# Digit codes for the one-hots, first picks among the last dense tiles, other shares of weighing, six dot products handed over

## The chip, the cores and the metric

The kernel runs on one core of a Trainium2 chip. The time is device microseconds of one execution, and the metric is the median over runs. Engine names are those of the profile: PE is TensorE (PEld its weight loads), DVE is VectorE, ACT is ScalarE, POOL is GpSimd, and SP is SyncE, which here only issues DMAs.

## What is computed

One layer on 256 tokens of width 2048: a modulated norm, an input projection, an RWKV-7 group beside a short convolution, an output projection, and then the PEER feed-forward, a mixture of 16,384 tiny experts. Only the last is touched:

```python
v1, i1 = lax.top_k(s1, PEER_TOPK)                # 16 of 128 first keys, per token and head
v2, i2 = lax.top_k(s2, PEER_TOPK)                # 16 of 128 second keys
cidx = i1[..., :, None] * N_KEYS + i2[..., None, :]
top, pos = lax.top_k(cand, PEER_TOPK)            # 16 experts of 8 heads: 128 per token
gate = jax.nn.softmax(top, axis=-1)
u = jnp.take(expert_u, idx, axis=0)
act = jax.nn.gelu(jnp.einsum('td,tkd->tk', h_t, u), approximate=False)
vv = jnp.take(expert_v, idx, axis=0)
return jnp.einsum('tk,tkd->td', g * act, vv)
```

## The kernel before

All work is written out by hand, engine by engine, with semaphores; each engine runs its own list in order. The feed-forward goes through four stages.

**Dense u stage.** Each expert row u has 2048 columns. The first 896 are multiplied densely for all experts: 128 tiles (`u_dense`, 448 KB each), tile j holding the experts whose second key is j, seven matmuls per tile (L1330); ACT copies each result to `dense` (L842). SP loads the tiles (`product_tile`, L450): ten of them (`KEPT`) early into spare memory, the others into four slots, each load waiting for the product that frees its slot. The other 1152 columns are fetched by gather: POOL issues one indirect DMA for each of 256 rows n = (block of 128 tokens, k) (L599) into a ring of six slots, and gather n waits until `u_dot` says that dot n-6 is done. DVE routes (`route`) and makes the dots (`dots`, L1794), 198 of them (`LATE`) before it turns to the next stage.

**Pick stage.** 64 iterations q of four tokens. PE spreads the four tokens' first keys over the partitions (`spread_keys`, L1344, four bf16 matmuls), ACT makes of them a one-hot with two operations (`one_hot`: Abs L857, Relu L859), PE multiplies the one-hot with `dense` (`key_rows`, L1356) and transposes it (`turn_one_hot`, L1363), ACT keeps the transposed one (L868), and DVE picks the products from PSUM (`pick`, L1802, four). In 58 of the iterations DVE also makes one of the remaining dots. Once block 0 is picked (q = 32), gelu and gate give its weights. From q = 36 on DVE, and in parallel POOL, write weighted one-hots for group q-36 (`weigh`, L1847 and L615, two tokens of four each; in block 1, POOL one of four), PE multiplies them in iteration q = group + 37 (`token_weights`, L1385), and ACT stores the result (L873). PE's order in an iteration is `spread_keys(q+1)`, `key_rows(q)`, `turn_one_hot(q)`, `token_weights(q-37)`. POOL's part of group j stands behind gather 232+j (`WEIGH_AT`), so it is issued after dot 226+j.

**Drain.** After the 64 iterations: groups 27 to 63 of the weighing, without picks.

**Dense v stage.** 128 tiles of `v_dense` (1104 columns) are multiplied on PE (L1413) while DVE sums 256 gathered rows of the other 944 columns (L1863).

## Time and profile before

| | |
|---|---|
| median of 3 runs | 1931.37 us (1931.03 to 1933.72) |
| the profiled execution's own time | 1930.16 us |
| its span, first to last instruction | 1928.4 us |
| busy: PE, DVE, ACT, POOL | 1833.6, 1317.2, 389.7, 750.5 us |
| mean granted clock of PE | 0.985 |
| HBM | 315 GB/s over the span |

The profile gives, per group of instructions, busy time, mean duration, and the idle time before them with what ended it; a chain that ended last; timelines; and busy time by windows. A busy share is a mean over stages, so the stages are read one by one.

### The profile page before, as it was taken

The numbers are of one execution on the slowest core, as the hardware profiler recorded it, in microseconds if no ns is written. First come the engines' busy times: TensorE is split into PE (matmuls) and PEld (weight loads), VectorE is DVE, ScalarE is ACT, GpSimd is POOL, SyncE is SP. The second block draws the span as 40 slices with busy tenths as digits, with TensorE's granted clock in tenths as the row PEclk, the third lists the DMA queues.
The fourth block names the chain that finished last, engine by engine and source line by source line (L and its number), as shares of the span: only waits on it lengthen the run. The fifth ranks groups of instructions, "written<-read, shape, count | busy, mean of one in ns | idle before, by whom it ended". The sixth has DMA issues, their size and how long they took to land.

```text
span 1928.4 us, 28418 instructions
## 1 busy us (share of the span) xinstructions
PE 1833.6 (95%) x10929; PEld 1415.7 (73%) x10929; DVE 1317.2 (68%) x2611; ACT 389.7 (20%) x842; POOL 750.5 (39%) x789
## 2 busy tenths in 40 slices
PE   3899999999999999999999999888989999999997
PEld 3787787777875458888888888778876666656664
DVE  5855666666662333598999975799986666666666
ACT  3022222222222020011111111588740000000001
POOL 2002212222111000365444443338895786744552
PEclk8789999999999999999999999999999999999999
DMA  9956656765581954989999999876449999999997
GB/s 396 420 200 263 228 197 248 292 249 210 213 345 54 402 204 157 370 323 410 405 407 402 402 410 409 327 230 205 144 154 408 409 409 408 409 408 409 409 406 284
DMA packets 124382, 609.09 MB, mean 316 GB/s; under 512 B 15584, under 2 KB 15712, under 8 KB 101216
## 3 DMA queue, kind: packets, MB, share of 16 engines
q1 hardware_dynamic: 66496, 330.33, 44.0%
q0 software_dynamic: 57344, 274.76, 37.3%
q8 instruction: 87, 1.43, 0.3%
q10 hardware_dynamic: 416, 2.25, 0.3%
q14 instruction: 39, 0.32, 0.0%
HBM read 603.09 MB, written 4.19 MB: 315 GB/s over the span
## 4 chain that ended last, share of the span: by engine, by line
PE 81%; DVE 8%; DMA 7%; issue 2%; POOL 2%; ACT 1%; DVEq 0%; SPq 0%; ACTq 0%
PE ps L1413 22%; PE ps L1330 20%; PE ps L996 14%; PE ps L1045 6%; PE ps L1235 6%; DMA arena<-in_v_dense 3%; PE ps L1084 3%; DVE arena L1474 2%; DVE ps L1802 2%; PE ps L1385 2%; DVE arena L1794 2%; DMA arena<-in_ada 2%; POOL arena L615 2%; DMA arena<-in_w_in 1%; PE ps L1356 1%
## 5 line engine op out<-in xcount | busy, mean ns | idle before, releaser
L1413 PE MATMUL ps<-arena 128*128 128x368 f32 x1536 | 477.4, 473 | 7.7 <-DMA arena<-in_v_dense 7.0
L1413 PEld LDWEIGHTS ps<-arena 128*128 128x128 f32 x1536 | 300.9, 196 | 182.8 <-DMA arena<-in_v_dense 10.9
L1863 DVE SCALAR_TENSOR_TENSOR arena<-arena 128x944 f32<-128x944 f32 x254 | 305.2, 1201 | 173.7 <-DMA arena<-in_v_rows,arena 172.3
L599 POOL DMA_INDIRECT arena<-in_u_rows,arena x256 | 257.6, 1006 | 346.6 <-DVE arena L1794 287.2
L1330 PE MATMUL ps<-arena 128*128 128x256 f32 x1792 | 386.9, 379 | 0.0
L1330 PEld LDWEIGHTS ps<-arena 128*128 128x128 f32 x1792 | 340.5, 190 | 46.1
L599 POOL DMA_INDIRECT arena<-in_v_rows,arena x256 | 295.7, 1155 | 182.3 <-DVE arena L1863 149.4
L996 PE MATMUL ps<-arena 128*128 128x256 f32 x1440 | 349.4, 386 | 2.6 <-DMA arena<-in_w_in 2.6
L1794 DVE SCALAR_TENSOR_TENSOR arena<-arena,ps 128x1152 f32<-128x1152 f32 x208 | 277.8, 1349 | 52.8 <-DMA arena<-in_u_rows,arena 52.2
L996 PEld LDWEIGHTS ps<-arena 128*128 128x128 f32 x1440 | 261.8, 190 | 40.6 <-DMA arena<-in_w_in 4.2
L1453 DVE SCALAR_TENSOR_TENSOR arena<-arena 128x2048 f32<-128x2048 f32 x60 | 143.5, 2392 | 24.8 <-DMA arena<-in_ada 24.7
L842 ACT ACTIVATE arena<-ps 128x256 f32<-128x256 f32 x128 | 52.0, 406 | 336.6 <-PE ps L1330 336.6
L1045 PE MATMUL ps<-arena 128*128 128x512 f32 x256 | 115.4, 598 | 0.0
L1235 PE MATMUL ps<-arena 128*128 128x256 f32 x512 | 111.4, 379 | 0.0
L1235 PEld LDWEIGHTS ps<-arena 128*128 128x128 f32 x512 | 96.9, 190 | 13.0
L725 ACT ACTIVATE arena<-ps 128x256 f32<-128x256 f32 x152 | 55.7, 383 | 200.9 <-PE ps L1084 139.0
L572 POOL TENSOR_TENSOR arena<-arena 128x256 f32<-128x256 f32 x40 | 39.1, 978 | 130.7 <-PE ps L1084 95.0
L1356 PE MATMUL ps<-arena 128*128 128x128 f32 x512 | 72.2, 281 | 12.7 <-DVE ps L1802 9.9
L1045 PEld LDWEIGHTS ps<-arena 128*128 128x128 f32 x256 | 47.0, 190 | 50.5 <-issue 49.4
L1474 DVE SCALAR_TENSOR_TENSOR arena<-arena 128x512 f32<-128x512 f32 x112 | 75.0, 745 | 10.6 <-DMA arena<-in_ada 10.4
L615 POOL TENSOR_SCALAR arena<-arena 128x128 f32<-128x128 f32 x96 | 78.1, 822 | 8.4 <-PE ps L1385 6.6
L1084 PEld LDWEIGHTS ps<-arena 64*64 64x64 f32 x2112 | 50.4, 133 | 39.6 <-issue 35.0
(251 smaller groups left out, 1746.0 us busy)
## 6 DMA issues: line engine op xcount, KB each, us to landing
arena<-in_ada SPq DMA_DIRECT2D x96, 1024.0 KB, 7.4
arena<-in_v_dense SPq DMA_DIRECT2D x128, 552.0 KB, 8.7
arena<-in_u_dense SPq DMA_DIRECT2D x128, 448.0 KB, 7.1
arena<-in_w_in SPq DMA_DIRECT2D x45, 1024.0 KB, 7.3
arena<-in_w_tail SPq DMA_DIRECT2D x32, 1024.0 KB, 9.1
arena<-in_w_in SPq DMA_DIRECT2D x12, 512.0 KB, 16.6
arena<-in_u_rows,arena POOLq DMA_INDIRECT x256, 10.1
arena<-in_v_rows,arena POOLq DMA_INDIRECT x256, 11.7
```

Source lines behind the costliest of these rows:

```text
L599: nc.gpsimd.indirect_dma_start(out=row, out_offset=None, in_=table[:, :], in_offset=bass.IndirectOffsetOnAxis(ap=i32(idx[:, b, k:k + 1]), ...
L615: last = nc.gpsimd.tensor_scalar(pick_w[q % len(pick_w)][i], iota, idx2T[:, t:t + 1], wT[:, t:t + 1], ALU.is_equal, ALU.mult)
L996: last = mm(bank(b, 0, T), w[:, k, :], hT[:, k, :], start=(k == 0), stop=(k == KC - 1))
L1045: return mm(bank(OUT_BANKS[g][b]), yT[:, OUT_K[n], b * P:(b + 1) * P], w, start=(n == 0), stop=(n == KC - 1))
L1084: last = mm(out(w, a, q), l(HALVES[w], a, q), r(HALVES[w], a, q), start=True, stop=True)
L1235: last = mm(bank(b0 + s // 2, (s % 2) * T, (s % 2) * T + T), w[:, kk, s * P:(s + 1) * P], h2T[:, k, :], start=(k == 0 and s % 2 == 0), sto ...
L1330: last = mm(bank(5 + j % 2, 0, T), w[:, k, :], h2T[:, k, :], start=(k == 0), stop=(k == KU - 1))
L1413: last = mm(sums(b)[:, g, :], dense[:, b, j // 2, :, j % 2], w[:, g * VG:(g + 1) * VG], start=(j == 0), stop=(j == NKEYS - 1))
L1453: ins = stt(dst, ring[:, slot, :], silu_c[:, k:k + 1], dst, ALU.mult, ALU.add)
L1474: v0.done(stt(a, row, silu_c[:, k:k + 1], a, ALU.mult, ALU.add), name)
L1794: stt(row, row, 1.0, h, ALU.mult, ALU.mult, accum_out=actv[:, b, k:k + 1]).then_inc(u_dot, 1)
L1863: stt(total[b], row, w, total[b], ALU.mult, ALU.add).then_inc(v_sum, 1)
```

## The change

In words, part by part:

- **Codes.** The first key is written as two digits (hi = key/16, lo = key mod 16) and their squares, in bf16: `make_digits` on DVE (eight small operations per block), saved to a DRAM tensor `first_key_codes` by two ACT DMAs before tile 112's copy. `code_tile(q)` on SP loads them back, 4 partitions x 4 x 256 bytes, one DMA per iteration, 64 in all, into two code tiles of eight used rows. One matmul with constant weights (`code_w`, made on POOL; bias by `make_bias` on DVE) and one Relu now give the one-hot. SP's list has the code tiles behind the last u tile and ahead of the first v tile; the v tiles also wait for `handed_sum`.
- **First picks.** PE transposes the second keys and does `spread_keys(0)` ahead of u tile 125, ACT copies them and makes one-hot 0 before the copy of tile 126, and the eight Exp of the gates stand before the copy of tile 112.
- **Kept tiles.** 14 instead of 10; six of these are loaded among the output projection's tiles.
- **Dots.** `LATE` is 202 instead of 198, and the pick stage holds 48 dots instead of 58: none in q = 0, 1, 5, 8, ..., 29, 31, 40, 47, 54, 61.
- **Handed dots.** The last six rows (k = 122 to 127 of block 1) are gathered by POOL into two other buffers, multiplied there with a copy of h (`h_copy`, ACT, in q = 1), and summed by ACT (q = 12, 17, ..., 37).
- **Weighing.** POOL's parts of groups 0 to 31 stand behind gathers 232 to 249, five for every four gathers; in block 1, POOL has one token in two groups of three and none in the third, where DVE does all four. The transpose of block 0's weights moves from q = 34 to 35.

PE at the end of the u tiles, before (L1330 tile products, L1335 second keys, L1344 spread, L1356 key rows, L1363 transposes):

```order
L1330 MATMUL ps<-arena 128x256 [waits u_tile_evacuated,u_tile_landed3]
L1330 MATMUL ps<-arena 128x256 x6
L1330 MATMUL ps<-arena 128x256 [waits u_tile_evacuated,u_tile_landed0]
L1330 MATMUL ps<-arena 128x256 x6
L1330 MATMUL ps<-arena 128x256 [waits u_tile_evacuated,u_tile_landed1]
L1330 MATMUL ps<-arena 128x256 x6
L1335 MATMUL ps<-arena 128x128 [waits experts_picked]
L1335 MATMUL ps<-arena 128x128
L1344 MATMUL ps<-arena 128x128 [waits u_row_multiplied]
L1344 MATMUL ps<-arena 128x128 x3
L1344 MATMUL ps<-arena 128x128 [waits one_hot_ready]
L1356 MATMUL ps<-arena 128x128 [waits one_hot_ready,u_tile_evacuated]
```

And the same place now (L1434 tile products, L1424 second keys, L1418 spread, L1446 key rows):

```order
L1424 MATMUL ps<-arena 128x128 [waits experts_picked]
L1424 MATMUL ps<-arena 128x128
L1418 MATMUL ps<-arena 128x512 [waits first_key_code_landed0,first_key_code_landed1,numbers_made,u_row_multiplied]
L1434 MATMUL ps<-arena 128x256 [waits u_tile_evacuated,u_tile_landed3]
L1434 MATMUL ps<-arena 128x256 x6
L1434 MATMUL ps<-arena 128x256 [waits u_tile_evacuated,u_tile_landed0]
L1434 MATMUL ps<-arena 128x256 x6
L1434 MATMUL ps<-arena 128x256 [waits u_tile_evacuated,u_tile_landed1]
L1434 MATMUL ps<-arena 128x256 x6
L1418 MATMUL ps<-arena 128x512 [waits one_hot_ready]
L1446 MATMUL ps<-arena 128x128 [waits one_hot_ready,u_tile_evacuated]
```

Three tile products now stand behind a matmul that waits for two code tiles to land. SP's list there, now (before, the v tiles followed the u tiles at once):

```order
L452 DMA arena<-in_u_dense 128x896 [waits u_tile_product] x110
L508 DMA arena<-first_key_codes 4x4x128 [waits first_key_digits_saved,code_tile_zeroed]
L508 DMA arena<-first_key_codes 4x4x128 x3
L508 DMA arena<-first_key_codes 4x4x128 [waits first_keys_spread]
L508 DMA arena<-first_key_codes 4x4x128
...
L517 DMA arena<-in_v_dense 128x1104 [waits u_tile_product,handed_row_summed]
```

The code tiles are issued behind every u tile. POOL from gather 227 on, now (L631 gathers, L673 weighing, two tokens a group):

```order
L682 TENSOR_TENSOR arena<-arena 128x1152 [waits handed_row_landed1]
L631 DMA arena<-in_u_rows,arena 128x1152 [waits u_row_multiplied] x6
L673 TENSOR_SCALAR arena<-arena 128x128 [waits turned_weights_evacuated]
L673 TENSOR_SCALAR arena<-arena 128x128
L631 DMA arena<-in_u_rows,arena 128x1152 [waits u_row_multiplied]
L673 TENSOR_SCALAR arena<-arena 128x128 x2
```

Group j's weighing on POOL still starts behind gather 232, as before; but the dot that gather 232 waits for has moved. DVE's list around its first weighing (group 0, q = 36), before:

```order
L1794 SCALAR_TENSOR_TENSOR arena<-arena,ps 128x1152 [waits u_row_landed5]
L1802 SCALAR_TENSOR_TENSOR ps,arena<-arena,ps 128x128 [waits key_rows_ready]
L1802 SCALAR_TENSOR_TENSOR ps,arena<-arena,ps 128x128 x3
L1794 SCALAR_TENSOR_TENSOR arena<-arena,ps 128x1152 [waits u_row_landed0]
L1847 TENSOR_SCALAR arena<-arena 128x128 [waits turned_weights_evacuated]
L1847 TENSOR_SCALAR arena<-arena 128x128
```

and now:

```order
L1914 SCALAR_TENSOR_TENSOR arena<-arena,ps 128x1152 [waits u_row_landed3]
L1922 SCALAR_TENSOR_TENSOR ps,arena<-arena,ps 128x128 [waits key_rows_ready]
L1922 SCALAR_TENSOR_TENSOR ps,arena<-arena,ps 128x128 x3
L1914 SCALAR_TENSOR_TENSOR arena<-arena,ps 128x1152 [waits u_row_landed4]
L1974 TENSOR_SCALAR arena<-arena 128x128 [waits turned_weights_evacuated]
L1974 TENSOR_SCALAR arena<-arena 128x128
```

Row n lies in slot n mod 6: the dot ahead of weighing 0 was number 228 (slot 0) and is now number 226 (slot 4). The core of the diff:

```diff
@@ SP
+                if n in EARLY_KEPT:
+                    keep_tile(EARLY_KEPT[n])
...
+            def code_tile(q):
+                b, t = divmod(4 * q, P)
+                if q == 0:
+                    sp.wait_ge(code_zero, 2)
+                    sp.wait_ge(digits_saved, 16 * TB)
+                if q >= 4 and q % 2 == 0:
+                    sp.wait_ge(spread, q - 2)
+                rows = code[q // 2 % 2][4 * (q % 2):4 * (q % 2) + 4, :]
+                sp.dma_start(rows.rearrange("r (t k) -> r t k", t=4), codes[b, t:t + 4].rearrange("t r k -> r t k")).then_inc(code_land[q % 4], 16)
+            for q in range(T // 4):
+                code_tile(q)
+            sp.wait_ge(handed_sum, HANDED)
@@ POOL
+            def hand(i):
+                if i:
+                    pool.wait_ge(handed_land[(i - 1) % 2], 16 * ((i - 1) // 2 + 1))
+                    row = handed_row[(i - 1) % 2]
+                    nc.gpsimd.tensor_tensor(row, row, h_copy, ALU.mult).then_inc(handed_mul, 1)
+                else:
+                    pool.wait_ge(tile_ps, NKEYS)
+                    pool.wait_ge(h_kept, 1)
+                if i < HANDED:
+                    if i >= 2:
+                        pool.wait_ge(handed_sum, i - 1)
+                    gather(handed_row[i % 2], u_rows, 1, KTOP - HANDED + i, handed_land[i % 2])
...
-                if n >= WEIGH_AT:
-                    weigh(n - WEIGH_AT)
+                if n in HAND_AT:
+                    hand(HAND_AT.index(n))
+                while n >= WEIGH_AT and weighed < min(5 * (n - WEIGH_AT + 1) // 4, P // 4):
+                    weigh(weighed)
+                    weighed += 1
@@ ACT
-                h = hot[q % 2].rearrange("p a b -> p (a b)")
-                nc.scalar.activation(h, bank(0), ACT.Abs, bias=minus_p).then_inc(hot_out, 1)
-                act.wait_ge(hot_out, 2 * q + 1)
-                nc.scalar.activation(h, h, ACT.Relu, bias=ones[:, 0:1], scale=-1.0).then_inc(hot_out, 1)
+                nc.scalar.activation(hot[q % 2].rearrange("p a b -> p (a b)"), bank(0), ACT.Relu, bias=one_minus).then_inc(hot_out, 1)
...
+                if q == 1:
+                    act.wait_ge(tile_ps, NKEYS)
+                    act.wait_ge(u_dot, LATE)
+                    nc.scalar.activation(h_copy, ps[:, GU:2 * GU], ACT.Copy).then_inc(h_kept, 1)
@@ PE
+            def spread_keys(q):
+                if q % 2 == 0:
+                    for n in range(2):
+                        pe.wait_ge(code_land[(q + n) % 4], 16 * (q // 4 + 1))
+                if q:
+                    pe.wait_ge(hot_out, q)
+                mm(bank(0), code_w[q % 2], code[q // 2 % 2], start=True, stop=True).then_inc(spread, 1)
@@ tables
-LATE = TB * KTOP - 58
-KEPT = tuple(24 + 6 * n for n in range(10))
+HANDED = 6
+NROWS = TB * KTOP - HANDED
+LATE = 202
+NO_DOT = (0, 1) + tuple(range(5, 32, 3)) + (31,) + (40, 47, 54, 61)
+HAND_AT = tuple(LATE + UROWS + 3 * i for i in range(HANDED + 1))
+SUM_AT = tuple(12 + 5 * i for i in range(HANDED))
+KEPT = tuple(18 + 6 * n for n in range(14))
+EARLY_KEPT = {8: 2, 10: 3, 12: 4, 14: 5, 16: 12, 18: 13}
...
-WEIGH_AT = TB * KTOP - 24
-POOL_TOKENS = ((2, 3), (3,))
+WEIGH_AT = 232
...
+def pool_tokens(q):
+    return (2, 3) if q < P // 4 else (3,) if q % 3 else ()
```

## Rows read from the trace of the kernel before

**Rows 1.** Busy time by windows: stretch, length, PE, PEld, DVE, ACT, POOL, clock, DMA, GB/s.

```profile
1100.00:1200.00 100.00, 100.00 (x465) 88.06 (x464) 68.98 (x125) 13.34 (x33) 40.28 (x43) 1.00 1.03 409
...
1260.00:1280.00 20.00, 16.77 (x154) 15.29 (x151) 20.00 (x91) 17.66 (x30) 7.36 (x8) 1.00 0.74 221
...
1340.00:1360.00 20.00, 19.11 (x170) 17.55 (x169) 20.00 (x85) 16.61 (x29) 18.55 (x22) 1.00 0.69 207
...
1500.00:1600.00 100.00, 100.00 (x385) 63.69 (x384) 65.05 (x55) 1.09 (x2) 82.37 (x55) 1.00 1.02 408
```

**Rows 2.** The chain that ended last, two pieces: start us, us, what.

```profile
840.96 386.79 PE ps L1330 x1792
...
1433.65 59.63 PE ps L1413 x192
```

**Rows 3.** Timeline, last dot ahead and first pick: start, us, engine, line, [idle before].

```profile
1224.97 1.35 DVE L1794 SCALAR_TENSOR_TENSOR arena<-arena,ps 128x1152 f32<-128x1152 f32 x1
...
1227.77 0.40 ACT L842 ACTIVATE arena<-ps 128x256 f32<-128x256 f32 x1 [2.62 <-PE ps L1330]
...
1230.84 1.13 PE L1356 MATMUL ps<-arena 128*128 128x128 f32 x8 [0.44 <-ACT arena L859]
...
1232.09 0.35 DVE L1802 SCALAR_TENSOR_TENSOR ps<-arena,ps 128x128 f32<-128x128 f32 x1 [5.76 <-PE ps L1356]
```

**Rows 4.** Timeline of SP's queue, the last six u tile loads.

```profile
1200.57 15.44 SPq L450 DMA_DIRECT2D arena<-in_u_dense  x6
```

**Rows 5.** DMA view, 1222 to 1223 us, SP's queue q1: packets, MB, share.

```profile
q1 hardware_dynamic: 2, 0.00, 1.0%
```

**Rows 6.** DMA view, 710 to 845 us: SP's store of x, KB, us to landing.

```profile
out<-arena SPq DMA_DIRECT2D x1, 2048.0 KB, 16.9
```

**Rows 7.** Timeline of DVE in an early iteration: first pick, dot, next pick.

```profile
1272.34 0.35 DVE L1802 SCALAR_TENSOR_TENSOR ps<-arena,ps 128x128 f32<-128x128 f32 x1
...
1273.42 1.35 DVE L1794 SCALAR_TENSOR_TENSOR arena<-arena,ps 128x1152 f32<-128x1152 f32 x1
...
1274.69 0.35 DVE L1802 SCALAR_TENSOR_TENSOR ps<-arena,ps 128x128 f32<-128x128 f32 x1
```

**Rows 8.** Timeline of one iteration with weighing, all engines.

```profile
1321.18 1.02 POOL L599 DMA_INDIRECT arena<-in_u_rows,arena  x1 [0.17 <-issue]
...
1321.49 1.35 DVE L1794 SCALAR_TENSOR_TENSOR arena<-arena,ps 128x1152 f32<-128x1152 f32 x1
...
1322.24 1.64 POOL L615 TENSOR_SCALAR arena<-arena 128x128 f32<-128x128 f32 x2
...
1322.77 0.59 DVE L1847 TENSOR_SCALAR arena<-arena 128x128 f32<-128x128 f32 x2
...
1323.29 0.34 DVE L1802 SCALAR_TENSOR_TENSOR ps<-arena,ps 128x128 f32<-128x128 f32 x1
...
1323.47 1.13 PE L1385 MATMUL ps<-arena 128*128 128x128 f32 x8
...
1324.66 1.11 PE L1356 MATMUL ps<-arena 128*128 128x128 f32 x8
```

**Rows 9.** Timeline, a dot and the gather that waited for it.

```profile
1305.04 1.35 DVE L1794 SCALAR_TENSOR_TENSOR arena<-arena,ps 128x1152 f32<-128x1152 f32 x1
...
1306.67 0.94 POOL L599 DMA_INDIRECT arena<-in_u_rows,arena  x1 [1.41 <-DVE arena L1794]
```

**Rows 10.** Timeline, multiplications of 256 columns on POOL, and DVE beside one.

```profile
417.09 2.34 DVE L1453 SCALAR_TENSOR_TENSOR arena<-arena 128x2048 f32<-128x2048 f32 x1
...
417.25 2.77 POOL L579 TENSOR_TENSOR arena<-arena 128x256 f32<-128x256 f32 x1 [0.36 <-DVE arena L1606]
...
420.09 0.61 POOL L581 TENSOR_TENSOR arena<-arena 128x256 f32<-128x256 f32 x1
```

**Rows 11.** Timeline, one-column matmuls of PE.

```profile
710.02 3.85 PE L929 MATMUL ps<-arena 128*128 128x1 f32 x32
```

**Rows 12.** Windows as in Rows 1: granted clock just behind.

```profile
713.00:717.00 4.00, 4.00 (x23) 4.00 (x23) 3.13 (x8) 2.55 (x9) 0.00 (x0) 0.57 0.99 371
```

More of the change, by code:

```diff
@@ L242, in build_layer @@
         idx2T = new(T)
-        ident_h = new(P // 2).bitcast(BF16)
-        idx1_h = [new(KTOP // 2).bitcast(BF16) for _ in range(TB)]
         actv, wv = new(TB, KTOP), new(TB, KTOP)
+        digit_at = [take(0) - TB * KTOP, take(2 * KTOP)]
+        digits = [view(a, 2 * KTOP).bitcast(BF16).rearrange("p (t k) -> p t k", t=4) for a in digit_at]
+        code_w = [ones[:, n * KTOP // 2:(n + 1) * KTOP // 2].bitcast(BF16) for n in range(2)]
         assert take(0) <= ring_at + 3 * SL
@@ L630, in _ @@
                 if n == 0:
-                    for q in range(TB * KTOP - WEIGH_AT, P // 4):
+                    for q in range(weighed, P // 4):
                         weigh(q)
@@ L1894, in _ @@
                     keep_weights(0)
[L1895 removed]
+                if q not in NO_DOT:
                     dots(ndot[0], ndot[0] + 1)
```

214 lines of the change are left out of this document (148 added, 66 removed).

## The prediction

> **What bounds the kernel now.** I read the chain that ended last first, then busy time by windows, then the timelines at the joints. The chain is PE's nearly everywhere: the u tiles are one unbroken piece of 386.79 us, 3.022 us a tile, from 840.96 to 1227.75, and the v tiles start at 1433.65 [rows 2]. The reader should see in the windows which stage leaves which engine room [rows 1]. In the u stage PE and the DMA engines are both full (409 GB/s) and DVE is idle for 31 of 100 us. In the early iterations of the pick stage DVE is full, at 20.00 of 20, and PE, ACT and POOL are not. In the iterations with weighing DVE is full, PE has 0.9 us left of 20 and POOL 1.5. In the v stage PE and DMA are full and the change touches nothing. So only the 205.9 us between the last u tile and the first v tile can move, and whatever delays a u tile is paid in full; the v stage follows with its 487 us unchanged, since its bytes, slots and order are the same.
>
> **Where the picks begin.** Between the last u tile and the first pick lie 4.3 us, in which DVE sits idle for 5.76 us and PE and ACT work on one-hot 0 [rows 3]. With one-hot 0 ready, what is left is ACT's last copy (0.40), the signal to PE (0.15) and the key rows (1.25 from start to pick): 1.8 us, a gain of 2.5. The first two iterations then have no dot, which takes 2 x 1.27 us from DVE [rows 7], but it can't use this: one-hot 2 stands on ACT behind the new copy of h, 1152 columns from PSUM, and pick 2 comes about 6.2 us after the last u tile against 9.1 now. Both together: **-2.9 us**.
>
> **Codes.** PE now waits ahead of tile 125 for code tiles 0 and 1. PE is there at 840.96 + 125 x 3.022 = 1218.7. SP issues them behind the last u tile, so not before 1216.0 [rows 4], and the last u tile's bytes leave SP's queue only at about 1222, after which it is empty [rows 5]. That a small transfer doesn't pass what stands ahead of it in SP's queue is seen earlier: the 2 MB store needs 16.9 us to land [rows 6], although 2 MB alone are 5 us at 409 GB/s, because four query tiles of 1 MB each stand ahead. So the codes land between 1222.1 and 1224; I take 1223.2, near the queue's end since they are small. With signal and spread (0.4 us) tile 125 starts at 1223.6 instead of 1218.7: **+4.9 us**, bounds 3.9 and 6.0 if the queue holds. PE is then idle for 4.5 us. Behind the nearest stretch of this kind, 3.85 us of one-column matmuls [rows 11], the granted clock fell to its lower level (1.2 GHz) and was 0.57 on average over the next 4 us [rows 12], that is some 3.4 us at half rate: **+1.7 us**, bounds 0 and 1.7; I take the upper end because the idle stretch is longer than that one.
>
> By the Trainium skill (DMA: Bandwidth & Descriptors, "Anatomy of one DMA") a transfer costs about 2.0 us plus its bytes, and by that alone the codes would land at about 1218.2 and PE would wait for nothing. The same page ("Queues, rings and completion order") says that each DMA engine takes the descriptors of a ring in order; by that rule, the trace agrees with its 16.9 us.
>
> **Dots.** An iteration with a dot takes DVE 1.08 us of picks and 1.27 of dot [rows 7]; with weighing, dot and two tokens take 1.80 [rows 8], in all 2.87. In iterations 2 to 31 there were 24 dots and are 20, and DVE is the full engine: 4 x 1.27 = **-5.1 us**. In block 1 four more iterations lose their dot, but there PE is full for 19.11 of 20 us, 2.74 of 2.87 [rows 1], and DVE must wait for its key rows: 0.13 each by the windows, at most about 0.3 by PE's gaps, **-1.0 us** with bounds -0.5 and -1.3. The four dots moved ahead of the picks bring 4 x 0.59 MB into the u stage and the four more kept tiles take 4 x 0.46 MB out of its DMA-bound part: 0.5 MB, 1.3 us at 409 GB/s. The last dot ahead of the picks ended at 1226.3 [rows 3] and ends near 1227.6, while PE's first picks aren't ready before 1234. Nothing, unless PE doesn't wait. The bias, digits and clearing on DVE (some 30 small operations, 6 us) lie in its idle 31 per cent. The six early kept tiles (6.6 us of DMA) load among the output projection's tiles, where PE has six slots ahead. The Relu that replaces two operations, and the one spread matmul for four, free ACT and PE, which aren't full in the early iterations: nothing.
>
> **Weighing on POOL.** This is the largest term. POOL's part of group j stands behind gather 232+j (five groups for four gathers), and gather n waits for dot n-6. Before, dot 226 was made in iteration 34 and group 0 was needed by PE in iteration 37. Now `LATE` is 4 higher, but 12 of the first 32 iterations have no dot instead of 6: dots 202 to 221 fill iterations 2 to 30, dot 222 falls on 32, and dot 226 on 36. So POOL can start on group 0 only behind the dot of iteration 36, and PE wants it in iteration 37, ahead of the key rows of iteration 38, for which DVE waits. The loop of two iterations is: gather starts 0.28 after the dot ends [rows 9], gather 1.02, two tokens 1.64, signal about 0.14 (an estimate, half of the 0.28), PE's weighing and spread 1.19 (1323.47 to 1324.66), key rows to pick 1.25, picks 1.08, dot 1.35 [rows 3, 7, 8], in all 7.95 us, against 2 x 2.87 = 5.74 us now. That is 2.2 us for every pair of groups whose POOL part has only one iteration's lead. Counted through the order, with five groups for four gathers and no dot at 40, 47, 54 and 61, those groups are 0, 1, 2, 3, 5, 6, 7, 8, 12 and 13; the others have two iterations and are on time. Five pairs: **+11.0 us**, bounds 8 (if some of the wait fits PE's gaps) and 13.
>
> **Handed dots.** Six multiplications of 1152 columns on POOL: 4.5 x 0.61 = 2.75 us each by the row without interference [rows 10], while POOL is busy for 7.4 of 20 us [rows 1]. Three rows take DVE 3 x 2.35 and one and a half iterations without a dot 1.6, 8.7 us, and POOL's work for them is 3 x 1.2 + 2.75 = 6.4. Hidden; uncovered from 5 us a multiplication. ACT's copies and sums (seven of about 1.2 us) lie in what the dropped Abs frees.
>
> **Drain.** POOL's share of block 1 falls to two thirds and DVE's rises by 11 tokens of 0.26 us; PE needs 0.90 us a group either way. I take -0.4, bounds 0 and -1.
>
> **Sum.** -2.9 + 4.9 + 1.7 - 5.1 - 1.0 + 11.0 - 0.4 = +8.2 us. The profiled execution, 1930.16 us, becomes 1938.4; the median lies 1.2 us above that execution, so the forecast is 1931.37 + 8.2 = **1939.6 us**. With all lower or all upper bounds at once: 1933 to 1944.
>
> **The rivals.** *The codes land in time*, because small descriptors get through between those of the u tile. For it: code tiles are 16 KB. Against it: [rows 6]. Then the 4.9 and 1.7 us go: 1933.0. *POOL is early enough*, because its lead is longer than I count. For it: POOL has slack in the early iterations. Against it: gather 232 can't be issued before its dot whatever POOL's slack. Then 1928.6. *Both*, which is the case on the other side: it decides at the point where the two delays together are below the 9.4 us that the picks gain, and with neither the time is 1939.6 - 17.6 = 1922.0, faster. *POOL's multiplications are held up by DVE*: one of 256 columns took 2.77 us instead of 0.61 while DVE worked on two operands in SBUF [rows 10]. Against it: the dots take one operand from PSUM, and POOL's weighing beside them kept its 0.82 us a token [rows 8]. At 8 us each, 6 x (3.6 + 8 - 8.7) = 17 us more: 1957. The Trainium skill (SBUF — State Buffer, "SBUF: two separate sides") says that a DVE operation with two SBUF inputs and a GpSimd operation exclude each other for their whole length; by that rule, the trace agrees with the 2.77 us, and the dots wouldn't hold POOL up.
>
> **How the numbers follow.** Forecast 0.50, codes in time 0.11, POOL early 0.16, both 0.15, multiplications held up 0.06, and 0.02 for the rest. The range takes in the forecast with its bounds and the second and third case, and leaves out most of the last two: 1925 to 1945. A measurement of this kernel tells about 0.2% (3.9 us) from no change. The cases at 1933.0 and 1928.6 lie within it, the latter not far from its edge: faster 0.18, same 0.25, slower 0.57.
>
> **What would show it.** A wait of 4 to 6 us of PE ahead of tile 125, ended by a DMA of the codes, and the granted clock behind it. First pick 1.8 us after the last u tile. Early iterations at 2.35 us with a dot and 1.08 without. Ten iterations from q = 36 to 49 in pairs of 7.9 us, with PE's weighing waiting for POOL (L673). The forecast is wrong if the u tiles end before 1229, or if PE never waits more than a few us in all for POOL's weighing.

## The result, and the profile after

The changed kernel takes 1946.92 us (median; 1945.24 to 1948.72) and the kernel before 1931.3 us beside it: the medians lie 15.6 us apart. The ratio is 1.0074 with a 95% interval of 1.0061 to 1.0087, which is 14.3 us. The forecast was 1939.6 us with a range of 1925 to 1945. The direction was right, the forecast change of 8.2 us was about half of what came, and the time lies 1.9 us above the range.

The profiled execution of the changed kernel has a span of 1945.9 us against 1928.4, 17.5 us more. The chain that ended last has again one piece per stage, but there is now a transfer in it (start us, length us, what; L1434 are the u tiles' products, L1476 the token weights, L1502 the v tiles):

```profile
839.46 374.70 PE ps L1434 x1736
1214.98 7.56 DMA arena<-first_key_codes
1223.27 11.51 PE ps L1434 x42
...
1449.79 59.63 PE ps L1502 x192
```

The u tiles, one piece of 386.79 us in [rows 2], are broken by a code tile of 4 KB that lands 7.56 us after it was issued (at 1222.54), and the three tiles behind it take 11.51 us, where three tiles before took 9.07. The v tiles start at 1449.79 instead of 1433.65. PE's timeline (start us, us, [idle before and what ended it]) and then the windows (columns as in [rows 1]; the eighth number is the granted clock) show both:

```profile
1217.01 0.38 PE L1424 MATMUL ps<-arena 128*128 128x128 f32 x2
1222.68 0.59 PE L1418 MATMUL ps<-arena 128*128 128x512 bf16 x1 [5.29 <-DMA arena<-first_key_codes]
1223.06 11.70 PE L1434 MATMUL ps<-arena 128*128 128x256 f32 x42
```

```profile
1220.00:1223.00 3.00, 0.32 (x1) 0.33 (x2) 2.05 (x5) 0.00 (x0) 1.20 (x2) 0.70 1.04 410
1223.00:1226.00 3.00, 3.00 (x8) 2.40 (x8) 2.87 (x5) 0.00 (x0) 2.01 (x3) 0.50 1.02 407
```

PE stood idle for 5.29 us; then it is busy for 3.00 of 3.00 us with 8 matmuls, at the lower level of its clock (0.50), where a window of the same length at 1.00 holds 15.

The first picks answer to [rows 3]. The last u tile ends at 1234.78 (1223.27 + 11.51); the picks of iterations 0, 1 and 2 (picks 0, 1 and 2 from here on) start 1.7, 3.2 and 5.7 us later, against 4.3, 6.7 and 9.1 before. On DVE's timeline:

```profile
1236.52 0.35 DVE L1922 SCALAR_TENSOR_TENSOR ps<-arena,ps 128x128 f32<-128x128 f32 x1 [9.78 <-PE ps L1446]
...
1237.99 0.36 DVE L1922 SCALAR_TENSOR_TENSOR ps<-arena,ps 128x128 f32<-128x128 f32 x1 [0.24 <-PE ps L1446]
...
1240.45 0.36 DVE L1922 SCALAR_TENSOR_TENSOR ps<-arena,ps 128x128 f32<-128x128 f32 x1 [1.24 <-PE ps L1446]
```

The handed multiplications, which [rows 10] could only scale to 2.75 us, are one group of the view by lines for 1240 to 1320 us (count, busy us, mean ns):

```profile
L682 POOL TENSOR_TENSOR arena<-arena 128x1152 f32<-128x1152 f32 x6 | 15.9, 2658 | 0.9 <-DMA arena<-in_u_rows,arena 0.8
```

Where weighing begins, the timeline reads quite unlike [rows 8]. L1914 is DVE's dot, L631 the gather, L673 POOL's weighing, L1476 PE's use of it, L1446 the key rows that DVE's next pick (L1922) needs:

```profile
1316.01 1.60 POOL L673 TENSOR_SCALAR arena<-arena 128x128 f32<-128x128 f32 x2
...
1317.66 2.07 PE L1476 MATMUL ps<-arena 128*128 128x128 f32 x8 [5.02 <-POOL arena L673]
...
1319.96 1.91 PE L1446 MATMUL ps<-arena 128*128 128x128 f32 x8
...
1321.91 0.36 DVE L1922 SCALAR_TENSOR_TENSOR ps<-arena,ps 128x128 f32<-128x128 f32 x1 [3.75 <-PE ps L1446]
...
1322.99 1.35 DVE L1914 SCALAR_TENSOR_TENSOR arena<-arena,ps 128x1152 f32<-128x1152 f32 x1
...
1324.62 0.99 POOL L631 DMA_INDIRECT arena<-in_u_rows,arena  x1 [4.08 <-DVE arena L1914]
...
1325.66 1.57 POOL L673 TENSOR_SCALAR arena<-arena 128x128 f32<-128x128 f32 x2
...
1327.28 0.97 PEld L1476 LDWEIGHTS ps<-arena 128*128 128x128 f32 x8 [1.87 <-POOL arena L673]
1327.28 1.16 PE L1476 MATMUL ps<-arena 128*128 128x128 f32 x8 [1.63 <-POOL arena L673]
...
1328.49 1.05 PE L1446 MATMUL ps<-arena 128*128 128x128 f32 x8
...
1329.59 0.35 DVE L1922 SCALAR_TENSOR_TENSOR ps<-arena,ps 128x128 f32<-128x128 f32 x1 [1.37 <-PE ps L1446]
```

Read from 1322.99 down, this is the loop that the prediction named: dot, gather (which had waited 4.08 us for it), two tokens on POOL, PE's weighing, the key rows, the next pick. Above it is the same loop with PE at half clock: its weighing takes 2.07 us instead of 1.16 and the key rows 1.91 instead of 1.05. The granted clock of that stretch, and PE's waits for POOL from 1300 to 1410 us (total us, times, longest):

```profile
1317.60:1321.90 4.30, 4.24 (x19) 4.08 (x20) 0.56 (x4) 1.18 (x2) 2.61 (x4) 0.50 0.72 242
```

```profile
PE ps L1476 <- POOL arena L673: 17.5, 11, 5.0
```

The starts of the first picks of all iterations, taken from DVE's timeline, give the whole pick stage. Iterations 37 and 38 take 10.04 us together, 39 and 40 take 7.70, 42 and 43 take 7.71, 44 and 45 take 8.88, 49 and 50 take 8.89, against 5.74 before: 14.5 us more in ten iterations. The others with weighing take 2.9 with a dot and 2.5 without, but for 57 to 60 with 3.0 to 3.2. The two pairs of 7.7 us have the clock at 1.00 throughout, although PE waits 2.55 us for POOL in one of them (first window below). In the pair of iterations 44 and 45 it falls 1.5 us after PE has resumed its work at 1346.05, behind a wait of 2.09 us (second window):

```profile
1338.40:1342.00 3.60, 3.40 (x27) 3.13 (x28) 1.75 (x11) 1.77 (x3) 2.61 (x3) 1.00 0.71 239
1347.60:1350.90 3.30, 3.30 (x18) 3.30 (x17) 1.94 (x9) 1.41 (x3) 2.86 (x4) 0.50 0.60 179
```

From the profiled execution of before to that of after, in us:

| stretch | before | after | change | forecast |
|---|---|---|---|---|
| start of the u tiles | 840.96 | 839.46 | -1.5 | 0 |
| u tiles, with the wait for the codes | 386.79 | 395.3 | +8.5 | +6.6 |
| last u tile to pick 2 | 9.05 | 5.67 | -3.4 | -2.9 |
| pick 2 to pick 36 | 75.03 | 71.88 | -3.1 | -5.1 |
| pick 36 to pick 63 | 78.06 | 91.77 | +13.7 | +10.0 |
| pick 63 to the first v tile | 43.76 | 45.69 | +1.9 | -0.4 |
| v tiles to the end | 494.75 | 496.1 | +1.4 | 0 |
| sum | | | +17.5 | +8.2 |

### The profile page after: what moved, and what is told of

Same layout as the page of the kernel before. It is cut to its first block, busy times and chain, and to the rows that moved or that the text cites. A ratio compares the mean times of both kernels' runs of the same rounds, so it can differ in the third digit from the quotient of the medians.

```text
span 1945.9 us, 28104 instructions
## 1 busy us (share of the span) xinstructions
PE 1835.6 (94%) x10737; PEld 1414.1 (73%) x10737; DVE 1315.7 (68%) x2624; ACT 355.5 (18%) x791; POOL 786.1 (40%) x798
## 4 chain that ended last, share of the span: by engine, by line
PE 79%; DMA 8%; DVE 7%; issue 2%; POOL 2%; ACT 1%; DVEq 0%; SPq 0%; another core or an unknown queue 0%; ACTq 0%
PE ps L1502 22%; PE ps L1434 20%; PE ps L1083 13%; PE ps L1132 6%; PE ps L1322 6%; DMA arena<-in_v_dense 3%; PE ps L1171 3%; PE ps L1476 3%; DMA arena<-in_ada 2%; DVE arena L1563 2%; DVE ps L1922 2%; DMA arena<-in_w_in 1%; DVE arena L1914 1%; PE ps L1446 1%; POOL arena L673 1%
## 5 line engine op out<-in xcount | busy, mean ns | idle before, releaser
L1502 PE MATMUL ps<-arena 128*128 128x368 f32 x1536 | 477.4, 473 | 7.9 <-DMA arena<-in_v_dense 7.2
L1502 PEld LDWEIGHTS ps<-arena 128*128 128x128 f32 x1536 | 300.7, 196 | 183.1 <-DMA arena<-in_v_dense 11.3
L631 POOL DMA_INDIRECT arena<-in_u_rows,arena x256 | 257.4, 1005 | 342.4 <-DVE arena L1914 280.3
L1434 PE MATMUL ps<-arena 128*128 128x256 f32 x1792 | 389.6, 381 | 0.0
L631 POOL DMA_INDIRECT arena<-in_v_rows,arena x256 | 320.1, 1251 | 159.2 <-DVE arena L1990 114.8
L1434 PEld LDWEIGHTS ps<-arena 128*128 128x128 f32 x1792 | 342.2, 191 | 47.0
L1914 DVE SCALAR_TENSOR_TENSOR arena<-arena,ps 128x1152 f32<-128x1152 f32 x202 | 269.4, 1350 | 46.2 <-DMA arena<-in_u_rows,arena 43.7
L1083 PEld LDWEIGHTS ps<-arena 128*128 128x128 f32 x1440 | 261.5, 190 | 41.6 <-DMA arena<-in_w_in 5.0
L1322 PEld LDWEIGHTS ps<-arena 128*128 128x128 f32 x512 | 96.9, 190 | 13.0
L1922 DVE SCALAR_TENSOR_TENSOR ps<-arena,ps 128x128 f32<-128x128 f32 x256 | 73.7, 351 | 29.8 <-PE ps L1446 28.6
L1476 PE MATMUL ps<-arena 128*128 128x128 f32 x512 | 69.6, 289 | 24.6 <-POOL arena L673 22.3
L1476 PEld LDWEIGHTS ps<-arena 128*128 128x128 f32 x512 | 64.4, 200 | 30.1 <-POOL arena L673 25.9
L1132 PEld LDWEIGHTS ps<-arena 128*128 128x128 f32 x256 | 46.9, 190 | 50.5 <-issue 49.4
```

The source lines that it names most:

```text
L631: nc.gpsimd.indirect_dma_start(out=row, out_offset=None, in_=table[:, :], in_offset=bass.IndirectOffsetOnAxis(ap=i32(idx[:, b, k:k + 1]), ...
L1083: last = mm(bank(b, 0, T), w[:, k, :], hT[:, k, :], start=(k == 0), stop=(k == KC - 1))
L1132: return mm(bank(OUT_BANKS[g][b]), yT[:, OUT_K[n], b * P:(b + 1) * P], w, start=(n == 0), stop=(n == KC - 1))
L1322: last = mm(bank(b0 + s // 2, (s % 2) * T, (s % 2) * T + T), w[:, kk, s * P:(s + 1) * P], h2T[:, k, :], start=(k == 0 and s % 2 == 0), sto ...
L1434: last = mm(bank(5 + j % 2, 0, T), w[:, k, :], h2T[:, k, :], start=(k == 0), stop=(k == KU - 1))
L1476: last = mm(bank(token_bank(q), i * P, (i + 1) * P), pick_w[q % len(pick_w)][i], dense[:, b, :, t, :], start=True, stop=True)
```

## The experiments

Every kernel was timed beside the kernel before on its own chip; ratios are to that. Not all ran on the same chip: the first four are from one chip (number 2 on record), the next three from a second (12), the last five from a third (3). Where stretches are compared, they are read from one profiled execution of each.

**Codes earlier** (one edit of the changed kernel):

```diff
                 if n >= len(u_tile):
                     sp.wait_ge(tile_ps, loaded[n - len(u_tile)] + 1)
+                    if j == NKEYS - 4:
+                        for q in range(4):
+                            code_tile(q)
                     product_tile(j)
```

> The changed kernel, with the four first code tiles issued by SP ahead of the load of tile 124 instead of behind the last u tile; nothing else differs. Theory A (the codes stand behind the u tiles' bytes in SP's queue, and PE's clock falls behind that wait): the wait of 5.3 us ahead of tile 125 and the 2.5 us by which the three last tiles are longer than 9.07 both go, 1946.9 - 7.8 = 1939.1 us. Rival B (the codes are small, but waited for because the digits' round trip through DRAM is late, or PE then waits for the u tile instead, since the DMA engines are full): the wait stays under another name, 1945 to 1947 us. My recorded terms (4.9 and 1.7) would give 1940.3 us.

Measured: 1939.65 us, ratio 1.0038 (1.0023 to 1.0052), 7 us less than the change. The u tiles take 388.6 us instead of 395.3. PE no longer waits for codes and its three last tiles take 9.08 us in the chain; but it waits 1.15 us for a u tile instead, since SP was late with that load by its four additional issues:

```profile
1217.26 3.29 PE L1437 MATMUL ps<-arena 128*128 128x256 f32 x14 [1.15 <-DMA arena<-in_u_dense]
```

Theory A holds (1939.1 us), with a small part of B behind it. The five long pairs are all still there (9.74, 7.68, 7.71, 8.88 and 8.93 us).

**POOL's weighing earlier** (one number of the changed kernel):

```diff
-WEIGH_AT = 232
+WEIGH_AT = 230
```

> The changed kernel with one number changed: POOL's part of weighing group 0 stands behind gather 230 instead of 232, the others accordingly. Theory A (POOL's lead is one iteration for ten groups, since gather 232 waits for the dot of iteration 36): all five long pairs of iterations go, which are 14.5 us longer than 5.74 each in the trace of the changed kernel (10.04, 7.70, 7.71, 8.88, 8.89), 1946.9 - 14.5 = 1932.4 us. My recorded term gives 1946.9 - 11.0 = 1935.9 us. Rival B (POOL is late because it has too much work beside the handed multiplications, not because of where the order puts it): the wait moves to the gathers and DVE's dots wait for rows instead, above 1943 us.

Measured: 1932.91 us, ratio 1.0007 (0.9998 to 1.0016): by the ratios 12.9 us less than the change, for a place two gathers earlier. Iterations 38 to 50 take 2.5 to 3.2 us each; iteration 37 takes 4.05. The wait for the codes is unchanged in its chain (1215.09, 7.67 us). In the profiled executions 12.1 us of the difference lie between picks 36 and 63 and 2.4 between picks 2 and 36, a stretch that the edit doesn't touch (more on it below). The first is the largest part of the loss, and it is the place in POOL's order that makes it; rival B, above 1943 us, is out.

**Both.**

> Codes ahead of tile 124 and weighing from gather 230, together. Theory A (the two terms are independent): 1946.9 - 7.8 - 14.5 = 1924.6 us, below the 1931.3 of the kernel before. By the recorded terms 1946.9 - 6.6 - 11.0 = 1929.3 us. Rival B (the gains overlap, as an engine with no room left takes over, PE first, which had 0.9 us of 20 left in the weighing iterations): 1928 to 1932 us.

Measured: 1925.67 us, ratio 0.9971 (0.9962 to 0.9980), and in a second set of runs (below) 0.9959 (0.9945 to 0.9973). The terms add up: by the ratios 7.0 + 12.9 = 19.9 us, and 19.9 measured, each uncertain by some 3 us. Rival B's 1928 us lies at the edge of the interval. With its two delays gone the change is 0.3 to 0.4% faster than the kernel before, which was the third rival of the prediction with its 1922.0. Iteration 37 takes 2.87 us here; most of 43 to 53 take 3.0 instead of 2.87, with DVE full, since its two tokens take 0.81 us instead of 0.59.

**No dots handed over.** The kernel with both early, with HANDED = 0, the copy of h and the six multiplications and sums left out, and these numbers:

```diff
-NO_DOT = (0, 1) + tuple(range(5, 32, 3)) + (31,) + (40, 47, 54, 61)
-WEIGH_AT = 230
+NO_DOT = (0, 1, 8, 14, 20, 26, 40, 47, 54, 61)
+WEIGH_AT = 236
```

> As the kernel with both early, but no dot product is handed to POOL and ACT: DVE makes all 256, six of the iterations without a dot get one again (10 iterations without), the copy of h, the six multiplications and the six sums are left out, and POOL's weighing starts behind gather 236, whose dot is made in iteration 34. Theory A (handing saves 6 x 1.27 = 7.6 us of DVE in the early iterations, and gives back 1.24 us at pick 2 behind the copy of h and 2.3 us in three iterations in which ACT's sum holds up the one-hots): 7.6 - 3.5 = 4.1 us slower than the kernel with both early, about 1928.7 us. Rival B (what it gives back is nothing, as the forecast had it): 7.6 us slower, 1932.2. Rival C (handing gives nothing because the early iterations are then held by the one-hots' loop between PE and ACT): equal to the kernel with both early, 1924.6.

Measured: 1932.43 us, ratio 1.0006 (0.9997 to 1.0015), 6.8 us above the kernel with both early. From pick 0 to pick 63 it takes 158.07 us against 151.37, 6.7 us more: six dots of 1.28 us, 7.7, less 0.9 at pick 2. That 0.9 is seen on DVE's timeline, first of this kernel, then of the one with both early, where the copy of h stands ahead of one-hot 2 on ACT:

```profile
1232.78 0.36 DVE L1918 SCALAR_TENSOR_TENSOR ps<-arena,ps 128x128 f32<-128x128 f32 x1 [0.33 <-PE ps L1444]
```

```profile
1234.31 0.35 DVE L1925 SCALAR_TENSOR_TENSOR ps<-arena,ps 128x128 f32<-128x128 f32 x1 [1.24 <-PE ps L1449]
```

Rival B is nearest. ACT's sums cost nothing: my theory A had put the late picks 12, 21, 24 and 30 of the changed kernel down to them, and they are not late in the kernel with both early, which makes the same sums.

**PE kept busy while it waits for the codes** (the changed kernel, with work that nobody reads):

```diff
                     pe.wait_ge(numbers, NUMBERS)
+                    for k in range(12):
+                        mm(bank(0, 0, T), h2T[:, k % KU, 0:P], h2T[:, k % KU, :], start=True, stop=True)
                     spread_keys(0)
```

> The changed kernel, in which PE, ahead of its wait for the codes, makes 12 more matmuls of the u tiles' shape from h into bank 0, which nobody reads and the first spread matmul overwrites: 12 x 0.43 = 5.2 us of work in place of a wait of 5.3 us. Theory A (the clock falls because PE stood idle): the granted clock stays at 1.00 behind the codes and the three last tiles take 9.07 us instead of 11.5, 1946.9 - 2.5 = 1944.4 us. Rival B (the clock falls for another reason, or PE is late because of the additional work): the three last tiles take 11.5 us as before, 1947 us, or up to 1948 if the added work ends after the codes have landed.

Measured: 1949.7 us, ratio 1.0079 (1.0066 to 1.0093), no gain in time. But its own stretch went as theory A said, whose time was 1944.4. PE's timeline, where L1429 is the added work, and the windows:

```profile
1218.86 5.34 PE L1429 MATMUL ps<-arena 128*128 128x256 f32 x24
1224.63 9.22 PE L1436 MATMUL ps<-arena 128*128 128x256 f32 x42 [0.42 <-DMA arena<-first_key_codes]
```

```profile
1223.00:1226.00 3.00, 2.58 (x13) 2.16 (x13) 2.80 (x5) 0.00 (x0) 1.55 (x2) 1.00 1.04 412
```

The clock stays at 1.00 and three tiles take 9.2 us instead of 11.7: the clock fell because PE stood idle. The time did not fall because in this trace other stretches are longer: pick 2 to pick 36 (73.6 us instead of 71.9), and the long pairs (9.59, 8.87, 9.22, 8.94 and 9.03 us), 45.6 in place of 43.2, with the clock falling in all five pairs instead of three. Whether the added work has a part in that, or it is the next execution's chance, isn't shown.

**POOL's share of block 1 as before** (the kernel with both early):

```diff
-    return (2, 3) if q < P // 4 else (3,) if q % 3 else ()
+    return (2, 3) if q < P // 4 else (3,)
```

> The kernel with both early (1925.7 us), with POOL's part of weighing block 1 as it was before the change: one token of every group, instead of one token in two groups of three; nothing else differs. My recorded term says that the new share gains 0.4 us of the drain: 1926.1 us. Theory A (in all four kernels with the new share the time from pick 63 to the first v tile is 45.6 to 46.5 us, against 43.76 in the kernel before, so the new share costs 1.9 to 2.7): 1923.0 to 1923.8 us, and PE's granted clock is 1.00 in the drain instead of 0.95. Rival B (the longer drain comes with the clock alone, which falls behind a wait that the share has nothing to do with): no change, 1925.7 us, and a clock of 0.95 again.

Measured: 1930.96 us, ratio 0.9988 (0.9979 to 0.9997), by the ratios 3.3 us above the kernel with both early, where my term said 0.4 above and theory A 1.9 to 2.7 below. Theory A is wrong in its clock too. But the two kernels ran on different chips, and what differs in their traces is mostly not in the drain, the only place where they have different instructions. The drain, from pick 63 to the first v tile, takes 45.4 us. Windows over the drain, of the kernel before, of this one, of the change, and of the one with both early:

```profile
1389.90:1433.60 43.70, 36.66 (x306) 34.91 (x306) 38.34 (x123) 24.66 (x41) 39.05 (x47) 1.00 0.24 69
```

```profile
1387.70:1433.00 45.30, 38.28 (x306) 36.52 (x306) 38.09 (x123) 24.62 (x41) 39.12 (x47) 0.96 0.24 67
```

```profile
1404.10:1449.80 45.70, 38.29 (x307) 36.54 (x307) 38.47 (x134) 24.68 (x41) 31.94 (x36) 0.96 0.25 72
```

```profile
1381.80:1428.20 46.40, 39.48 (x306) 37.90 (x306) 39.38 (x134) 24.64 (x41) 31.77 (x36) 0.93 0.24 72
```

The drain is as long as its clock is low, whatever the share: PE's busy time grows from 36.66 to 39.48 us for the same 306 matmuls. Over all fourteen traces it takes 43.8 to 44.1 us where the clock doesn't fall in it, 44.6 to 45.7 where it falls once, and 46.5 where it falls twice, with either share. Rival B holds for the drain. And the waits behind which it falls are not the change's. The kernel before waits for POOL in the same two places, and there its clock stays at 1.00:

```profile
1393.14 4.12 PE L1385 MATMUL ps<-arena 128*128 128x128 f32 x32 [1.64 <-POOL arena L615]
...
1400.97 5.63 PE L1385 MATMUL ps<-arena 128*128 128x128 f32 x48 [2.16 <-POOL arena L615]
```

The 3.3 us lie ahead of the drain, where this kernel and the one with both early have the same instructions: pick 2 to pick 36 takes 72.9 us against 69.5, in the iterations without a dot that are late in the change's trace too. DVE's timeline of the change shows one:

```profile
1262.67 0.35 DVE L1922 SCALAR_TENSOR_TENSOR ps<-arena,ps 128x128 f32<-128x128 f32 x1 [0.63 <-remote]
```

"remote" is no instruction of this program, and ACT stood idle over the same moment, for 0.76 us before 1262.73. I found no cause. The stretch takes 69.5 us in six traces (codes early, weighing early, both early twice, and the two below with a filled drain) and 71.9 to 73.6 in four (the change, PE filled, old share, combined); what sets it is open. One thing divides them: the last three of the four are all the runs of the second chip, the six are from the first and the third, and the kernel without handed dots, from the first, has no late pick either. The chip of the change's own trace isn't on record, and no kernel but the one before ran on the second chip and another. So the chip stands as a rival to the program, and what the share is worth in time isn't shown by this run.

**Combined** (both early, old share, WEIGH_AT = 231, and the four first code tiles one by one):

```diff
                     product_tile(j)
+                    if NKEYS - 8 < j <= NKEYS - 4:
+                        code_tile(j - (NKEYS - 7))
```

> The kernel with both early, with the old share of POOL in block 1, weighing from gather 231 instead of 230, and the four first code tiles issued one by one behind the loads of tiles 121 to 124 instead of four at once ahead of tile 124. Theory A: PE's wait of 1.2 us for a u tile at 1214.7 goes (SP was late with a load by the 1.35 us of the four issues), POOL weighs one gather later, so that its tokens lie less beside DVE's and iterations 43 to 53 take 2.87 instead of 3.00 (10 x 0.13), and the share brings 1.9 to 2.7: 1925.7 - 1.2 - 1.3 - 2.3 = 1920.9 us. Rival B (a lead of one gather less makes POOL late again in some groups): 1925 us or more. Rival C (only the share counts): 1923.4 us.

Measured: 1927.85 us, ratio 0.9971 (0.9962 to 0.9981). PE has no wait among the last u tiles, iterations 43 to 53 take 31.9 us instead of 32.6 and POOL is nowhere late, so A's first two parts hold in the trace, but the time is 7 us above its 1920.9; the share brings nothing in the drain, the late picks are there (72.1 us from pick 2 to pick 36), and the drain takes 46.5 us with the clock down twice. It ran on the second chip, so its ratio isn't held against that of the kernel with both early.

**Both early, again.**

> The kernel with both early, unchanged, so that it runs on the same chip as the two that follow, and so that the iterations without a dot are seen a second time. In its first trace picks 12, 21, 24 and 30 came 1.07 us after the pick before them; in the trace of the changed kernel and in those with the old share they came 1.2 to 1.9 us after. Theory A (that is the chip or the execution, not the program): its ratio to the kernel before is 0.997 within 0.002, and the picks may be late here too. Rival B (the old share slowed those kernels by itself): ratio 0.997 and no pick late here. Any further cost of the waits lies within 3 us.

Measured: 1924.41 us, ratio 0.9959 (0.9945 to 0.9973); no pick late (69.5 us). The same program took 2.87 us for iteration 37 in its first trace and 3.52 in this one, and 46.5 and 44.9 us for the drain. The clock falls twice in the drain of the first trace, at 1384.6 and 1394.9, and in the second once in the drain, at 1387.6, and once about iteration 37, at 1309.1. So neither the clock's falls nor the time that they cost are the same in two executions of one program. That no pick is late here doesn't tell chip from execution, since this was a third chip. The old share by itself (rival B) isn't what makes them late, as the change and the kernel with PE filled have the new share and late picks.

**PE kept busy in the drain** (both early, with work that nobody reads ahead of groups 27 and 32):

```diff
+            def keep_busy(n):
+                pe.wait_ge(turn_out, T // 4)
+                for _ in range(n):
+                    mm(bank(7, 0, P), ident, ident, start=True, stop=True)
...
+                if q == P // 4 - LAG:
+                    keep_busy(6)
                 token_weights(q)
+            keep_busy(9)
```

> The kernel with both early, and 6 and 9 matmuls of the identity by itself into a bank that nobody reads, ahead of the groups 27 and 32 of token weights, where PE waits 1.64 and 2.27 us for POOL. Theory A (PE's clock falls behind an idle stretch; both waits are followed by stretches at a granted clock of 0.5 in the trace of the kernel with both early): the clock stays at 1.00 in the drain, which takes 43.4 to 43.8 us instead of 46.5, and the time is 2.7 to 3.1 us below that of the kernel with both early, ratio to before 0.9955. Rival B (the added matmuls delay the groups): the same or up to 1 us longer.

Measured: 1924.66 us, ratio 0.9958 (0.9944 to 0.9971), the same as without (1924.41); the 2.7 to 3.1 us of theory A did not come. In its trace the drain takes 44.1 us at a full clock, where L1496 is the added work; the same place in the first trace without it comes second:

```profile
1387.42 1.50 PE L1496 MATMUL ps<-arena 128*128 128x128 f32 x12
1389.23 4.13 PE L1479 MATMUL ps<-arena 128*128 128x128 f32 x32 [0.31 <-POOL arena L676]
```

```profile
1385.00 5.38 PE L1479 MATMUL ps<-arena 128*128 128x128 f32 x32 [1.64 <-POOL arena L676]
```

32 matmuls take 4.13 us behind 0.31 us of idling and 5.38 behind 1.64. That the clock stayed up in the drain of this one trace doesn't show by itself that the filling did it, as the kernel before has a drain at 1.00 without any. As the drain without filling took 44.9 us in the execution beside it, about 1 us was to be had, and the timing doesn't tell that. With the codes one by one and weighing from 231 in addition:

> The same with filled waits in the drain, weighing from gather 231 instead of 230, and the four first code tiles one by one behind the loads of tiles 121 to 124; POOL's share is the new one. In the combined kernel with the old share PE had no wait among the last u tiles, and iterations 43 to 53 took 31.9 us together instead of 32.6. Theory A: 1.2 us for the u tiles and 0.7 us for the iterations less than the kernel with only the drain filled, ratio to before 0.9945. Rival B (the places of codes and weighing no longer matter): the same ratio as that one.

Measured: 1922.79 us, ratio 0.9953 (0.9939 to 0.9966), the fastest of all, 23.4 us below the change by the ratios; that it beats the one before it, by 1 us where theory A said 1.9, is within the intervals. The drain takes 44.1 us again, with no fall of the clock. Iterations 37 to 42 take 2.86 to 2.89 us with a dot, no pair is long, and no u tile waits.

**The lead of POOL in the kernel before** (one number, 24 to 23, then to 22):

```diff
-WEIGH_AT = TB * KTOP - 24
+WEIGH_AT = TB * KTOP - 22
```

> The kernel before with one number changed: POOL weighs group 0 behind gather 233 instead of 232, and one more group behind each further gather. Gather 233 waits for dot 227, made in iteration 35, and PE wants group 0 in iteration 37: the lead falls from three iterations to two, for all groups. Theory A (a lead of two iterations is enough, only one is too little): no change, 1931 to 1934 us. Rival B (every gather later costs the 1.02 us of a gather or more, since POOL is nearly full in these iterations): 1937 us or more.

> The same with gather 234, whose dot 228 is made in iteration 36: a lead of one iteration for all 22 groups that stand behind the gathers 234 to 255. Theory A (each pair of such iterations takes 7.7 us at full clock and up to 8.9 at a fallen one, instead of 2 x 2.87 = 5.74, as in the changed kernel): 11 pairs x 1.96 to 3.1 = 22 to 34 us more than the kernel before, 1954 to 1966 us. Rival B (in the changed kernel the lateness came from its handed rows and its groups of five to four gathers, and the place alone costs little): below 1945 us.

Measured: with a lead of two iterations 1932.86 us, ratio 0.9997 (0.9987 to 1.0006), iterations 36 to 58 at 2.86 or 2.87 us, as before; with a lead of one 1956.97 us, ratio 1.0134 (1.0112 to 1.0156). Iterations 37 and 38 take 8.96 us, with one fall of the clock, and from 39 to 58 they take 4.3 and 3.5 us in turn, ten pairs of 7.8 us. One turn of that loop, in the same order as above (L1794 dot, L599 gather, L615 POOL's weighing, L1385 PE's, L1356 key rows, L1802 pick):

```profile
1346.30 1.35 DVE L1794 SCALAR_TENSOR_TENSOR arena<-arena,ps 128x1152 f32<-128x1152 f32 x1
...
1347.93 1.03 POOL L599 DMA_INDIRECT arena<-in_u_rows,arena  x1 [0.83 <-DVE arena L1794]
...
1349.00 1.59 POOL L615 TENSOR_SCALAR arena<-arena 128x128 f32<-128x128 f32 x2
...
1350.64 1.16 PE L1385 MATMUL ps<-arena 128*128 128x128 f32 x8 [0.73 <-POOL arena L615]
...
1351.86 1.11 PE L1356 MATMUL ps<-arena 128*128 128x128 f32 x8
...
1353.01 0.36 DVE L1802 SCALAR_TENSOR_TENSOR ps<-arena,ps 128x128 f32<-128x128 f32 x1 [0.52 <-PE ps L1356]
```

Nothing of the change is in this kernel, neither handed rows nor five groups for four gathers, so the place alone makes the loop, and its threshold lies between two iterations and one. 11 x (7.8 - 5.74) = 22.7 us is what the loop gives; 23.7 us is what the profiled executions differ by from pick 0 to pick 63, and 25.9 (0.0134 x 1933.6) what the times do. Theory A's 1954 to 1966 us holds, and its rival is out.

## Why the prediction was right in direction and wrong in size

**Codes: mechanism right, mis-sized.** PE was to wait at tile 125 until SP's queue was empty, and did. The delay was 6.1 us (1223.27 instead of 839.46 + 125 x 3.022 = 1217.21), not 4.9, just beyond the bound of 6.0: counted from the start of the u tiles the codes landed 0.8 us later than forecast, and signal and spread took 0.7 us instead of 0.4. Each code tile is 4 KB, not the 16 KB that the first rival was given, and even so it didn't get through. The landing at about 1218.2, which stood beside the sum, did not come. The Trainium skill (DMA: Bandwidth & Descriptors, "Queues, rings and completion order") has each DMA engine take the descriptors of one ring in order; by that rule, the trace agrees with 7.56 us for 4 KB. The clock behind it cost 2.4 us (11.51 - 9.08), not 1.7.

**Where the picks begin: right.** -3.4 for -2.9; first pick 1.7 us after the last u tile for 1.8, pick 2 held up by ACT as told, at 5.7 instead of 6.2.

**Dots: right ahead of pick 36, but for something not foreseen.** From pick 2 to pick 36 the gain is 5.5 us in six traces (69.5 for 75.0: four dots and 0.4 in iteration 34), and 3.2 in the trace of the change. The 2.4 us between are the late picks that are left open. In block 1 three of the four iterations without a dot took 2.45 to 2.55 us, a gain of 0.4 where 0.13 to 0.3 was expected, and the fourth stands in a long pair and gained nothing. PE's busy 2.74 us of 2.87 was no bound: the kernel with both early begins one weighing on PE at 1315.46 and the next at 1317.97, 2.51 us later. With iterations 57 to 60 a little longer, all outside the long pairs came to -0.9 for -1.0.

**Weighing on POOL: mechanism and places right, mis-sized.** The ten groups named (0 to 3, 5 to 8, 12, 13) are the ten iterations that were long, and no other. (Of POOL's first 32 groups 22 stand behind the gathers 232 to 249, and the last ten follow them, which changes nothing here.) At full clock the loop took 7.70 us where 7.95 was worked out: 1.96 instead of 2.2 for a pair. But three of the five pairs took 10.04, 8.88 and 8.89, and those are the three in which PE's clock fell, behind waits of 5.02, 2.09 and 2.55 us. The prediction priced that for the codes and left it out here, one term further on, where it had the same wait of PE in hand: 5 x 1.96 = 9.8 us are the loop and 14.5 - 9.8 = 4.7 us the clock. That last part is read from which pairs have a fall and which don't, and over three traces it comes out without exception: with the codes early the same three pairs have a fall and take 8.9 to 9.7 us, the other two 7.7; with PE filled at the codes all five have one and take 8.9 to 9.6. Filling these waits wasn't tried.

**Handed dots: right.** 2.66 us for 2.75, hidden; the experiment without them gives their worth, 7.7 - 0.9 = 6.8 us. The rival in which DVE holds up POOL's multiplications fell: they took 2.66 us beside DVE's dots.

**Drain: wrong.** -0.4 became +1.9. At full clock the new share gains nothing (44.1 us with PE kept busy, 43.8 before with the old one, 0.3 us more): POOL's part of the chain that ended last falls from 71% of the drain to 45%, and PE's rises from 22% to 49%. The other 1.6 us are the clock (PE busy 38.29 us for 36.66 over the same matmuls). They are not the change's doing as far as is known: the waits stood there before, and the traces of the kernel before with a lead of two and of one have one fall in the drain as well (44.6 and 45.2 us).

**The step that failed** is thus the one that priced the clock behind PE's waits: it took one fall, +1.7 us behind the codes, as the whole of that cost, and put it at nothing in the weighing loop. The falls took 2.4 + 4.7 + 1.6 = 8.7 us in the trace, 7.1 of them behind waits that the change made. The 8.7 explain 7.0 of the 9.3 us by which the table's sum exceeds the forecast. The codes' wait (1.2), the late picks (2.4) and the drain's share (0.7) add to it; the loop's smaller size (1.2), the begin of the picks (0.5) and the early dots (0.4) take back some. What remains, -1.5 us at the start and +1.4 in the v stage, cancels by luck and is not the change's: over all traces shown here the u tiles start between 838.2 and 842.8 us and the v stage takes 494.6 to 496.1.

How far the time lies above the range, 1.9 us, is less than the late picks alone, whose cause is open; without them, or without the fall in the drain, it would have lain at the range's edge. The range's upper end, 1945, came of the bounds of the terms with a full clock in the loop; with the 4.7 us that the clock took there it would have been near 1950 and have held the time.

## What to carry to other kernels

When an instruction is moved ahead or behind in an engine's order, count its lead in turns of the loop that feeds it: a lead of two iterations cost nothing here and a lead of one made every pair of iterations 36% longer, at once and by one number. Wherever the sum lets PE wait for more than a microsecond or two, add what the clock may take behind it, place by place and as a chance (here 1.2 to 2.4 us, or nothing). And a small load that is issued behind large ones is a large load: issue it ahead of them, one at a time, so that the queue's own issue time delays none of them. (The traces show the waits gone; what the last 1.2 us are worth the times don't resolve.)

## What the hardware showed that was not expected

- **The clock falls behind short waits too, and not each time.** Behind 5.29 and 5.02 us of idling PE ran at a granted clock of 0.50 for 5.3 and 5.9 us. Behind 2.09 and 2.55 us it fell 1.4 to 1.5 us after PE had resumed, for 3.3 us; behind 1.64 us in the drain it fell at once in both traces of the kernel with both early. But behind 1.63 us in the loop, behind 2.55 us in another pair, and behind 1.64 and 2.16 us in the drain of the kernel before it stayed at 1.00. Work that nobody reads, put into the wait for the codes, kept it at 1.00 there.
- **A full clock gained in one place need not show in the time.** With PE kept busy at the codes the u tiles ended 1.5 us earlier, counted from their start, and the time did not fall: in that trace the long pairs took 2.4 us more and the stretch ahead of them 1.7.
- **DVE can stand for 0.6 to 0.7 us, at a few places of the early iterations, for something that the profile does not name**, in four traces and not in six others of programs with the same instructions there. The stretch took 2.4 to 4.1 us longer in the four. Three of them are all that ran on one chip, and chip and program are not told apart.
